# Two blocks of mixers on one core: input splits as own steps, attention divided before its turn, decay products moved from GpSimd to VectorE

## The reference, cut to what matters

```python
# SSD, two chunks of 128: L is the decay matrix, CB the products of C and B
y_diag = jnp.einsum('bcgls,bgecls,bcsgep->bclgep', CB, L, X)
...
# MLA: q and k from normed latents, 8 heads, a rotary part shared by the heads, two blocks of 128 queries
q = (rmsnorm(cq, q_norm_g) @ w_uq).reshape(Bsz, S, H, MLA_NOPE + MLA_ROPE)
kv = (rmsnorm(ckv, kv_norm_g) @ w_ukv).reshape(Bsz, S, H, MLA_NOPE + MLA_V)
pr = jax.nn.softmax(sc, axis=-1)
o = jnp.einsum('bhqk,bkhd->bqhd', pr, v)
...
mixed = g_ssd * (y_ssd @ w_ssd_out) + g_mla * (y_mla @ w_mla_out) + g_gdn * (y_gdn @ w_gdn_out)
h = x + mixed @ w_out
```

## Time and profile before

| | |
|---|---|
| median of 3 runs | 2849.06 us |
| the profiled execution, its own time | 2853.56 us |
| span of its core | 2851.3 us |
| granted TensorE clock, mean | 0.966 |
| TensorE matmul busy | 2705.2 us (95%) |
| VectorE, ScalarE, GpSimd busy | 1521.8, 1257.8, 412.7 us |
| mean share of the DMA engines | 37.3% in the weights' queue |

### The profile page before, as it was taken

One profiled execution on the slowest core, in us unless ns is written; L12 is line 12 of the kernel. 1 busy time (PEld: TensorE's weight loads), 2 busy tenths in 40 slices (PEclk: granted clock), 3 DMA queues, 4 the chain that ended last, 5 costly groups with the idle time before them and its releaser, 6 DMA issues.

```text
span 2851.3 us, 46221 instructions
## 1 busy us (share of the span) xinstructions
PE 2705.2 (95%) x20220; PEld 2493.3 (87%) x20220; DVE 1521.8 (53%) x2240; ACT 1257.8 (44%) x1877; POOL 412.7 (14%) x242
## 2 busy tenths in 40 slices
PE   7999998999999999999999999999999999999999
PEld 6999988889999998887899987578778999888999
DVE  3764457466546644565565523655333463766554
ACT  5734444445457334454454435654222453223543
POOL 4153110000042521100000000420000000331000
PEclk8999899999999998999999999999999999999999
DMA  4322334345534323343445333243333552212455
GB/s 156 127 96 89 133 119 148 133 148 181 189 139 140 110 89 114 124 144 137 163 169 184 131 111 131 90 157 125 133 133 115 203 185 103 74 60 76 171 185 176
DMA packets 56025, 384.28 MB, mean 135 GB/s; under 512 B 6032, under 2 KB 9744, under 8 KB 9872
## 3 DMA queue, kind: packets, MB, share of 16 engines
q1 hardware_dynamic: 55104, 376.14, 37.3%
q10 hardware_dynamic: 720, 5.18, 0.5%
HBM read 380.25 MB, written 1.05 MB: 134 GB/s over the span
## 4 chain that ended last, share of the span: by engine, by line
PE 81%; DVE 11%; ACT 5%; POOL 2%; issue 1%; DMA 0%; SPq 0%; DVEq 0%; ACTq 0%; POOLq 0%
PE ps L868 19%; PE ps L869 18%; PE ps L870 18%; DVE r L2008 3%; PE ps L829 2%; PE ps L1354 1%; PE ps L983 1%; PE ps L1060 1%; PE ps L1068 1%; PE ps L941 1%; PE ps L939 1%; PE ps L940 1%; ACT r L1412 1%; PE ps L904 1%; PE ps L905 1%
## 5 line engine op out<-in xcount | busy, mean ns | idle before, releaser
L868 PE MATMUL ps<-r,r 128*128 128x256 f32 (+1 forms) x4512 | 1362.2, 302 | 49.0 <-DVE r L2008 32.8
L869 PE MATMUL ps<-r,r 128*128 128x256 f32 (+1 forms) x4512 | 1346.5, 298 | 0.0
L870 PE MATMUL ps<-r,r 128*128 128x256 f32 (+1 forms) x4512 | 1345.5, 298 | 0.0
L2008 DVE TENSOR_TENSOR r<-ring,r 128x1024 fp32r<-128x1024 f32 (+2 forms) x558 | 684.8, 1260 | 520.9 <-ACT r L1412 520.7
L868 PEld LDWEIGHTS ps<-r,r 128*128 128x128 f32 x4512 | 870.1, 193 | 81.3 <-issue 32.7
L869 PEld LDWEIGHTS ps<-r,r 128*128 128x128 f32 x4512 | 869.6, 193 | 24.6 <-issue 1.0
L870 PEld LDWEIGHTS ps<-r,r 128*128 128x128 f32 x4512 | 868.8, 193 | 24.9
L1412 ACT ACTIVATE r<-ring 128x1024 fp32r<-128x1024 f32 (+1 forms) x614 | 613.8, 1039 | 286.8 <-DMA ring<-in_fi 64.7
L2816 POOL TENSOR_TENSOR slab<-slab 128x512 f32<-128x512 f32 (+1 forms) x20 | 28.1, 1407 | 1216.1 <-ACT slab L1535 1192.4
L2774 POOL TENSOR_TENSOR r<-ring,r 128x1024 fp32r<-128x1024 f32 x56 | 132.5, 2389 | 188.2 <-ACT r L1412 188.1
L2082 DVE SCALAR_TENSOR_TENSOR slab<-ps,v,slab 128x255 f32<-128x255 f32 (+1 forms) x168 | 67.5, 473 | 97.4 <-ACT slab L1489 97.3
(11 more groups left out here) (319 smaller groups left out, 3192.9 us busy)
## 6 DMA issues: line engine op xcount, KB each, us to landing
ring<-in_win SPq DMA_DIRECT2D x76, 1024.0 KB, 4.8
ring<-in_ada SPq DMA_DIRECT2D x48, 1024.0 KB, 4.8
ring<-in_fi SPq DMA_DIRECT2D x44, 1024.0 KB, 4.7
ring<-in_fo SPq DMA_DIRECT2D x36, 1024.0 KB, 4.7
ring<-in_wup SPq DMA_DIRECT2D x32, 1024.0 KB, 4.7
ring<-in_wdn SPq DMA_DIRECT2D x32, 1024.0 KB, 4.7
ring<-in_hin SPq DMA_DIRECT2D x20, 1024.0 KB, 4.7
ring<-in_nqkv SPq DMA_DIRECT2D x12, 1024.0 KB, 4.7
```

The costliest lines, as they stand in the source:

```text
L868: self.mm(o, hi[:, k - k0, cs], xh, k == 0, False)
L869: self.mm(o, hi[:, k - k0, cs], xl, False, False)
L870: i = self.mm(o, lo[:, k - k0, cs], xh, False, k == last)
L2008: self.tt(K.low(p), K.raw(p), K.high(p).bitcast(F32), ALU.subtract).then_inc(*self.up("w_lo_v", p))
```

## The change

- The split of an output projection's input is no longer the start of its job but a stream of its own, which `order1` places: `split wgo` behind the last step of `lat`, `split wso` behind the first step of `wuq`, `split wmo` in two halves (head pairs 0 and 1, then 2 and 3) behind the 8th and 10th step of the heads. One step of `ada0` and one of `gate_m` change places with others.
- The probabilities are divided before the turn: `divided` takes the reciprocal and multiplies both heads' exponentials in place (two tensor_scalar operations), and TensorE's turn waits for that, not for the exponentials. In step n VectorE does `divided` of pair n-1 ahead of the mask and maximum of pair n.
- The product with the values has its operands exchanged, so that the output stands features by rows; ScalarE copies it straight to `y`. The turns of the output, and the VectorE multiplication, are gone.
- The eight decay products of a layer are VectorE's, four behind Xs and four a step later; GpSimd's `ssd` is gone.
- The keys' latent is handled before the queries' in powers, logarithms, roots and norms, with one table load in place of two. The keys' rotary part moves to the first step of `mla`, with other scratch memory.

```diff
@@ memory
-        self.vt, self.PT, self.ot = A(2, 1024), A(8, 2, 128), A(8, 128)
+        self.vt, self.PT = A(2, 1024), A(8, 2, 128)
+        A.at += 1024
@@ order1
-    for fill in ("lat", "lat", None, "wgo", "wgo", ("mla", "wgo"), None, "wgo"):
+    for fill in ("lat", ("lat", "split wgo"), None, "wgo", "wgo", ("mla", "wgo"), None, "wgo"):
...
-                ("wuk", None), ("ada0", 1), ("ssd", 1), ("wuv", None), ("ssd", 1), ("ada0", 1), ("wuq", 1), ("ssd", None), ("wuq", None),
-                ("wso", 1), ("mla", 1), ("wso", 1)]
-    for n in range(10):
-        yield from [("mla", 1), (("wso", "wso", "gate_m", "ada0", "gate_m", "ada0", "ada0", "ada0", "gate_m", "gate_m")[n], 1)]
+                ("wuk", None), ("ada0", 1), ("ssd", 1), ("wuv", None), ("ssd", 1), ("ada0", 1), ("wuq", 1), ("ssd", None), ("wuq", 1),
+                ("split wso", 1), ("wuq", None), ("wso", 1), ("mla", 1), ("wso", 1)]
+    for fill in ("wso", "wso", "gate_m", "ada0", "gate_m", "ada0", "gate_m", ("split wmo", "ada0"), "ada0", "split wmo"):
+        yield ("mla", 1)
+        yield from [(name, 1) for name in ((fill,) if isinstance(fill, str) else fill)]
@@ TensorE.ssd
-                self.wait_ge(*at("sd_g", "L", L, c, 2 * g + 1))
+                self.wait_ge(*at("sd_v", "LC", L, c, 2 * g + 1))
@@ TensorE.mla
+        self.power_sum(("kn", L), 0)
         self.power_own(("qn", L))
         self.power_sum(("qn", L), 2)
-        self.power_sum(("kn", L), 0)
...
-            self.wait_ge(*at("ml_s", "e", L, i, hp))
+            self.wait_ge(*at("ml_v", "p", L, i, hp))
...
-                    m = mm(P[:, 128 * j:128 * j + 128], K.PT[:, 2 * s + j, kb, :], K.vt[:, kb, h * 128:h * 128 + 128], kb == 0, kb == i)
+                    m = mm(P[:, 128 * j:128 * j + 128], K.vt[:, kb, h * 128:h * 128 + 128], K.PT[:, 2 * s + j, kb, :], kb == 0, kb == i)
...
-            if hp == 3:
-                for g in range(2):
-                    P = self.open("ml_y", L, i, g)
-                    self.wait_ge(*at("ml_v", "o", L, i, 3))
-                    self.turn(P, [K.ot[:, 4 * g + j, :] for j in range(4)]).then_inc(*up("ml_p", "y", L, i, g))
@@ ScalarE
+    def split(self, job, parts):
+        src = job.more["source"]
+        for part in parts:
+            for i in part:
+                self.wait_ge(*self.have(job.more["source_at"](i)))
+                self.act(job.x[0][:, i:i + 2, :], src[:, i:i + 2, :], ACT.Copy).then_inc(*self.up("sp_s", job.key, i))
             yield
...
         def values(i, hp):
-            if hp == 3:
...
+            self.wait_ge(*at("ml_p", "o", L, i, hp))
+            self.act(K.y[:, hp:hp + 5:4, 128 * i:128 * i + 128], self.bank("ml_o", L, i, hp)[:, 0:256].rearrange("p (a b) -> p a b", a=2), ACT.Copy).then_inc(*up("ml_s", "y", L, i, hp))
@@ VectorE
+        def products(c):
+            for q in range(4):
+                D = K.L2[:, c, 4 * q:4 * q + 4, :]
+                self.wait_ge(*at("sd_s", "L", L, c, q))
+                self.wait_ge(*at("sd_v", "CB", L, c))
+                self.tt(D, D, bc(K.CB[:, c, q // 2:q // 2 + 1, :], [128, 4, 128]), ALU.mult).then_inc(*up("sd_v", "LC", L, c, q))
...
-        def values(i, hp):
+        def divided(i, hp):
             k0 = 8 * i + 2 * hp
             den = K.den[:, k0:k0 + 2]
             self.wait_ge(*at("ml_s", "e", L, i, hp))
             self.e.reciprocal(den, den).then_inc(*up("ml_v"))
             self.wait_ge(*mine("ml_v"))
-            self.wait_ge(*at("ml_p", "o", L, i, hp))
...
+            for j in range(2):
+                Pv = K.Pm[:, 2 * (hp % 2) + j, 0:128 * (i + 1)]
+                self.ts(Pv, Pv, den[:, j:j + 1], None, ALU.mult).then_inc(*up("ml_v"))
+            K.same("ml_v", ("p", L, i, hp))
...
         for n in range(len(steps) + 2):
+            if 1 <= n <= len(steps):
+                divided(*steps[n - 1])
             if n < len(steps):
                 scores(*steps[n])
-            if n >= 2:
-                values(*steps[n - 2])
             yield
```

More of the change, by code:

```diff
@@ L506, in jobs_block1 @@
         J["wuv"] = Job(("wuv", L), "wuv", L, range(2), 512, self.kn, xk(("kn", L)), "rows", to=[self.vt[:, m, :] for m in range(2)])
-        out("wmo", self.ys_m, "mix", source_at=lambda i: ("ml_s", ("y", L, 1, i // 4)), gate=self.gate, gate_of=("gate_m", L), first=False, split=self.ms)
+        out("wmo", self.ys_m, "mix", source_at=lambda i: ("ml_s", ("y", L, 1, i % 4 + 1)), gate=self.gate, gate_of=("gate_m", L), first=False, split=self.ms)
         mk = lambda k: ("ev_v", ("lo", ("wmo", L), k // 2))
@@ L682, in early @@
         yield
+    def split(self, job, parts):
+        yield from ()
     def follow(self, order):
@@ L708, in program @@
             self.streams |= {k: self.dense(j) for k, j in K.jobs1[L].items()}
+            self.streams |= {f"split {k}": self.split(K.jobs1[L][k], p) for k, p in (("wgo", [(0, 2, 4, 6)]), ("wso", [(0, 2, 4, 6)]), ("wmo", [(0, 4), (2, 6)]))}
             self.streams |= {"norm1": self.norm(("n1", L), L == 0), "angles": self.angles(), "small": self.small(L), "qk": self.qk(L),
@@ L1445, in dense @@
                 "relu2": self.relu2, "swiglu": self.swiglu, "forget": self.forget}[job.kind]
-        if "source" in job.more:
-            src = job.more["source"]
-            for i in range(0, 8, 2):
-                self.wait_ge(*self.have(job.more["source_at"](i)))
-                self.act(job.x[0][:, i:i + 2, :], src[:, i:i + 2, :], ACT.Copy).then_inc(*self.up("sp_s", job.key, i))
         for step in job.steps:
@@ L1458, in dense, with split @@
                     yield
+            yield
+    def split(self, job, parts):
+        src = job.more["source"]
[3 more added lines that the diff above has]
+                self.act(job.x[0][:, i:i + 2, :], src[:, i:i + 2, :], ACT.Copy).then_inc(*self.up("sp_s", job.key, i))
             yield
@@ L1583, in root @@
     def root(self, pid, rs, n, inv):
+        self.e.preload_act_table_set(LN_EXP)
         self.log(pid, rs, n, inv)
@@ L2039, in dense @@
                 "relu2": self.relu2, "swiglu": self.swiglu, "forget": self.forget}[job.kind]
-        if "source" in job.more:
-            src = job.more["source"]
-            for i in range(0, 8, 2):
-                self.wait_ge(*self.at("sp_s", job.key, i))
-                self.tt(job.x[1][:, i:i + 2, :], src[:, i:i + 2, :], job.x[0][:, i:i + 2, :].bitcast(F32), ALU.subtract).then_inc(*self.up("sp_v", job.key, i))
         for step in job.steps:
@@ L2052, in dense, with split @@
                     yield
+            yield
+    def split(self, job, parts):
+        src = job.more["source"]
+        for part in parts:
+            for i in part:
+                self.wait_ge(*self.at("sp_s", job.key, i))
+                self.tt(job.x[1][:, i:i + 2, :], src[:, i:i + 2, :], job.x[0][:, i:i + 2, :].bitcast(F32), ALU.subtract).then_inc(*self.up("sp_v", job.key, i))
             yield
@@ L2401, in ssd @@
         self.tt(heads(K.Xs), heads(K.Xd[:, 0, :]), bc(K.sc[:, 0, 0:16].unsqueeze(2), [128, 16, 64]), ALU.mult).then_inc(*up("sd_v", "Xs", L))
+        products(0)
         yield
@@ L2417, in ssd @@
                     self.emptied("sd_v", "sd_y", L, 1, g)
+            else:
+                products(1)
             yield
```

40 lines of the change are left out of this document (11 added, 29 removed).

## The result

The changed kernel takes 2824.2 us (median of 6 runs, 2817.3 to 2831.5), the one before 2850.0 beside it (6 runs, 2842.2 to 2854.8): a ratio of 0.991 with a 95% interval of 0.990 to 0.993. The forecast was 2823.0, range 2804 to 2839. Its profiled execution took 2831.5 where that of before took 2853.6.

A forecast was written before the change was run, and what follows sets the result against it. TensorE, 95% of the span, was held by waits and half clock behind them. Gains of 21.6 us less costs of 8.6 gave 13.0 a layer, 26 in both: 2827.6 profiled, 2823 as a median, range 2804 to 2839.

The forecast's parts named there:

- Split of wgo: First matmul of wgo in each layer: 3.0 of a 3.4 us wait goes, plus 2.5 us of clock, 5.5 gained.
- Xs: Scan's states: with GpSimd silent, TensorE's wait falls from 2.0 to 0.7 us, plus 1.5 of clock, 2.8 a layer.
- Keys first: Norms ahead of wuk: one table load less, 1.1 us a layer from a wait of 4.1; the order itself gives nothing.
- the rotary part: Keys' six rotary operations leave the chain before the scores: 1.8 us of wait and 3.0 of clock, 4.8 a layer.
- Turn of the output: Attention heads: 1.9 us of turn matmuls and two waits of 1.9 in all go, 3.8 a layer.
- Last turn: Turn of pair 7 waits 5.7 us for VectorE's queue and loses 2.5 of clock, a cost in each layer.
- first two: Turns of the first two head pairs: the mix of wso stands in front on VectorE, 0.2 us of wait each.
- Each figure below counts twice: Whole change: layer 1 shows the same waits within 0.1 us, so every figure for one layer was doubled.
- So that loss stays: At wuk: the remaining 3.0 us lie between waits that lost the clock, so the clock loss behind them stays.
- that the last turn does not wait: Rival, 14%: chunks ready before, or only copies in front counted; 8.3 us a layer come back, 2806.
- That the clock is not given back: Rival, 10%: without 1.5 and 3.0 of clock, and one more turn late, 3.7 us a layer remain: 2842.
- That five turns wait and VectorE's order bounds all heads: Rival, 5%: turns of pairs 0, 1, 2, 4 and 7 wait; each layer 5.8 us slower, 2861.

## Why the prediction was right, step by step

Net waits were right, term by term. **Split of wgo**: 3.4 to 0.2, forecast 3.0 of 3.4; undone, it comes back whole. **Xs**: 2.0 to 0.8, forecast 0.7; the cause, GpSimd beside VectorE, is shown by its undoing, and what is left is the copy of B, as forecast. **Keys first**: 4.1 to 3.0, forecast 3.0, and it is the table load. **wso** and **the rotary part**: gone, 1.5 and 1.8. **Turn of the output**: both waits gone; the 1.9 of its matmuls was not measured alone. **Last turn**: forecast 5.7, measured 5.9; **first two**: forecast 0.4 together, measured 0.8. All in all the steps summed to 12.7 less 6.1, 6.6 us less idle time a layer; the stage shows 6.3 and 5.9.

The clock was right in kind and mis-sized in four terms. The forecast gave it 4.5 a layer (2.5, 1.5 and 3.0, less 2.5); busy time fell by 4.9 and 4.0 us, which leaves 3.0 and 2.1 beside the 1.9 of turns. **"Each figure below counts twice"**: the waits are the same in both layers, the clock behind them is not. At `wgo` in layer 1 of the kernel before it was half for 3.4 us, 1.5 lost, and 2.5 was counted. **"Loses 2.5 of clock" at the last turn**: 9.5 us at half clock in the profiled execution, 4.2 lost, in both layers. In the profiles of five other kernels with the same wait of 5.9 us the stretch, idle time included, was 6.8 us in eight layers of ten and 13.7 in two. Where it was 6.8 it ended 3 to 4.7 us behind the turn's start, 1.3 to 2.0 lost. So 2.5 lies between the two prices, and the profiled execution, 7 us above its median, had the dear one in both layers. **"So that loss stays" at wuk**: it did not stay whole, 3.4 us at half in place of 6.8, 1.0 better. **Not in the sum at all**: the stretch at 530.4, 1.5 us, in both layers of the changed kernel, with no wait ahead of it. For layer 0: 13.0 - 1.7 + 1.0 - 1.5 - 0.3 of waits is 10.5, measured 11.2; for layer 1, with 1.0 less at `wgo`, 9.5, measured 9.9.

The term **"no turn of the output, 3.8"** hid how the change works. Its cost was forecast at 8.6 and came to 11.0 in the profiled execution (6.8 of waits, 4.2 of clock), but the two stood in separate paragraphs; taken together that part loses 4.8 a layer by the forecast's own terms. Alone on the kernel before it made the stage 3.0 and 4.0 longer, by another way: 2.6 of waiting at the last two turns and 10.2 us at half clock. The rest of the change carried it. The last turn that it made late was worth 13.5 us of median in one edit of VectorE's order. The 0.19 that the forecast estimates for a division was low: two took 0.62.

The rivals: that the last turn does not wait fell with its 5.9. That the clock is not given back fell, since it is full at all three places where the forecast had it back. That five turns wait and VectorE's order bounds all heads fell: turns 2 to 6 did not wait. That 2823 met 2824 by 1 us is partly luck. The sum said 26 us; the two profiled executions differ by 22.0 and the medians by 25.8. The forecast took the changed kernel's profile to lie 4.5 above its median, as before, and it lay 7.3 above, and that covered most of the 4 us by which the sum was too high.

What stays open: why the clock is half at 530.4 with TensorE busy throughout. The order does not decide it. The kernel with pair 7 divided early has the same instructions and waits up to that place and no such stretch in either layer, and in the one with `wmo`'s split later it stands in layer 0 and not in layer 1. No run was made for it alone. Nor was the exchange of `gate_m` and modulation steps undone by itself, only together with all else.

## What to carry to other kernels

When an operation is moved to another engine's stream, read what stands in front of it there and on the engine that feeds that; the price is that queue's, not the operation's (0.6 us of divisions, 5.9 of waiting), and often the order of one engine alone can be mended. Price a removed wait as itself plus what the clock loses behind it, read from rows at half clock, but keep that second part as a range over whole stretches: the stage of one kernel (GpSimd's products back) was 265.9 us in layer 0 and 272.2 in layer 1 with the same waits. For parts of a few us use the length of a stage in the profile, and a version whose clock is clean as the base: there one wait's price stands alone.

## What the runs showed of the hardware

- In every stage read here the half clock (1.2 GHz for 2.4) came in stretches of 3.4, 6.8, 10.2 or 13.7 us, whatever the length of the wait ahead. One of 3.4 costs 1.5 to 1.8 us where TensorE is busy throughout (busy time of the stage against 247.8 with none).
- The same wait of 2.3 us was followed by full clock in layer 0 and by 3.4 us at half in layer 1 of one execution; the rotary part's 1.8 us by 3.4 us at half in three places and by 6.8 in five. The 2.1 us at `wmo` in the kernel before were followed by full clock in both layers. A wait's clock price is not a constant of the wait.
- VectorE's operations on SBUF took 4.52 us for 2.35 and 2.28 for 1.22 while GpSimd's products ran, in both layers. Those with one operand in PSUM did not slow: a pair of 128x512 took 1.28 us with the products running and without.
- A second table load in a chain that was waited for cost 1.1 us, its own 1.28 less a wait that it hid; one that moved into the wait at `wmo` cost it whole (3.4 for 2.1).
- Two divisions (tensor_scalar of 128x256) took 0.62 us together, for the 0.25 each of the forecast.
